# Column tiles for the second mixer's output products in a one-core encoder layer

## The reference, cut to what matters

```python
for direction, reverse in ((0, False), (1, True)):
    lam_bar = jnp.exp(lam * step)
    b_bar = ((lam_bar - 1.0) / lam)[..., None] * b_in
    bu = jnp.einsum('blgi,gpi->blgp', ugc, b_bar)
    _, states = lax.associative_scan(
        _diag_recurrence, (jnp.broadcast_to(lam_bar, bu.shape), bu), axis=1, reverse=reverse)
    y = y + jnp.real(jnp.einsum('blgp,gip->blgi', states, c_out))
y = jax.nn.gelu(y.reshape(bsz, seqlen, S5_WIDTH))
```

## Time and profile before

| what | value |
|---|---|
| median of 3 runs | 3546.41 us (3544.83 to 3548.12) |
| the profiled execution | 3543.74 us |
| its span, first to last instruction | 3542.0 us |
| PE busy over the span | 3101.9 us, 88% |
| the stage `s5_outputs`, PE's first to last product | about 1376.5 to 1551.1 us |

### The profile page before, as it was taken

One profiled execution on the slowest core, in us unless ns is written; L12 is line 12 of the kernel. 1 busy time (PEld: TensorE's weight loads), 2 busy tenths in 40 slices (PEclk: granted clock), 3 DMA queues, 4 the chain that ended last, 5 costly groups with the idle time before them and its releaser, 6 DMA issues. The chain is left out here.

```text
span 3542.0 us, 41193 instructions
## 1 busy us (share of the span) xinstructions
PE 3101.9 (88%) x13052; PEld 1420.7 (40%) x13052; DVE 1339.5 (38%) x2344; ACT 751.0 (21%) x1652; POOL 675.4 (19%) x699
## 2 busy tenths in 40 slices
PE   8999999968799743978999965999999999999990
PEld 3444444436566402544444423333333333333330
DVE  3134223447688787623333344111111111111116
ACT  1011111123489500111212210111111111111116
POOL 1000000003255202413222220111111111111113
PEclk9999999988899876999999977999999999999995
DMA  6111020145344421462232114434545446344237
GB/s 242 48 54 65 36 77 30 42 142 170 114 137 141 182 89 45 130 212 107 99 116 116 59 49 184 139 99 118 161 112 148 116 117 189 88 145 118 53 101 291
DMA packets 147269, 414.96 MB, mean 117 GB/s; under 512 B 14421, under 2 KB 58197, under 8 KB 138597
## 3 DMA queue, kind: packets, MB, share of 16 engines
q1 hardware_dynamic: 108888, 315.88, 25.3%
q0 software_dynamic: 17024, 58.73, 8.3%
q10 hardware_dynamic: 21266, 39.16, 3.0%
HBM read 889.26 MB, written 122.16 MB: 286 GB/s over the span
## 5 line engine op out<-in xcount | busy, mean ns | idle before, releaser
L2218 PE MATMUL bank<-wg,exp_ht 128*64 128x512 f32 x1792 | 408.0, 597 | 1.1 <-DVE exp_ht L2307 1.1
L2218 PE MATMUL bank<-wu,exp_ht 128*64 128x512 f32 x1792 | 406.2, 595 | 1.3 <-issue 1.3
L2238 PE MATMUL bank<-wd,exp_hid_t 128*64 128x512 f32 x1792 | 395.8, 594 | 0.8 <-issue 0.8
L1669 PE MATMUL bank<-mix_wo,mix_yt 128*128 128x512 f32 x768 | 347.1, 602 | 18.2 <-DMA mix_wr<-in_w_router 10.6
L2173 POOL DMA_INDIRECT v<-exp_out,exp_sink x112 | 158.4, 1414 | 1003.8 <-DVE exp_out L2326 734.2
L472 PE MATMUL bank<-w_in,pro_ht 128*128 128x512 f32 x768 | 337.4, 592 | 0.0
L472 PE MATMUL bank<-pro_ht,w_in 128*128 128x512 f32 x768 | 336.4, 593 | 0.9 <-ACT pro_ht L534 0.9
L2318 DVE SCALAR_TENSOR_TENSOR exp_scale<-exp_g,row_gate,exp_scale 128x1024 f32<-128x1024 f32 x56 | 71.9, 1284 | 488.4 <-ACT exp_scale L2281 488.4
L2238 PEld LDWEIGHTS bank<-wd,exp_hid_t 128*64 128x64 f32 x1792 | 129.6, 137 | 257.0 <-issue 257.0
L2218 PEld LDWEIGHTS bank<-wg,exp_ht 128*64 128x64 f32 x1792 | 124.4, 137 | 233.0 <-issue 226.4
L2218 PEld LDWEIGHTS bank<-wu,exp_ht 128*64 128x64 f32 x1792 | 124.0, 137 | 232.4 <-issue 225.8
(11 more groups left out here) (348 smaller groups left out, 3974.5 us busy)
## 6 DMA issues: line engine op xcount, KB each, us to landing
wg<-in_w_gate SPq DMA_DIRECT2D x112, 2048.0 KB
wu<-in_w_up SPq DMA_DIRECT2D x112, 2048.0 KB
wd<-in_w_down SPq DMA_DIRECT2D x112, 2048.0 KB
ada_wt<-in_w_ada SPq DMA_DIRECT2D x8, 2048.0 KB, 10.5
pro_xt<-in_x SPq DMA_DIRECT2D x6, 2048.0 KB, 9.8
mix_xt<-in_x SPq DMA_DIRECT2D x6, 2048.0 KB, 12.8
v<-mix_kept_v ACTq DMA_DIRECT2D x24, 512.0 KB, 2.6
h<-mix_h ACTq DMA_DIRECT2D x24, 512.0 KB, 3.5
```

The source lines that it names most:

```text
L1669: mul = pe.matmul(C.bank[2 + 2 * (a % 2) + q][:, :], yt[:, j, k, a * P:(a + 1) * P], wo[:, k, q * WIDE:(q + 1) * WIDE], start=k == 0, stop ...
L2218: mul = pe.matmul(bank[rows, :], ht[:, j, k, rows], of[:, s, k * DE:(k + 1) * DE], start=k == 0, stop=k == KT - 1)
L2238: mul = pe.matmul(bank[rows, :], hid_t[:, j, k, rows], wd[:, s, k * D + q * WIDE:k * D + (q + 1) * WIDE], start=k == 0, stop=k == KD - 1)
```

## The change

It moves outputs to other partitions of PSUM, and changes the order of some loops:

- `kernel_of`: direction 1 goes to partitions 32 to 47 instead of columns 256 to 511, so that the two directions lie in two column tiles of 32. The loops go over `r`, then `d`, then `g` (before: `d`, `r`, `g`).
- `kernel_lags` reads direction 1 from there.
- `output`, prompt: the outputs of both groups go to one bank, group 0 on partitions 0 to 63 and group 1 on partitions 64 to 127, two column tiles of 64. In L1445 the two groups then differ in rows and in columns of the array; in L1455 (all 128 rows) they differ in columns. L1455 goes over `k`, then `g` (before: `g`, then `k`), for the sample too.
- gelu reads the prompt's outputs from there.

```diff
+    COL = 32
+        def bank_rows(i, g, s):
+
+            return yb[i * 2][g * C_P:(g + 1) * C_P, TC:2 * TC] if s else yb[i * 2 + g][0:C_S, 0:TC]
...
-                        f, b = kernel_bank[g][0:CH5, 0:TC], kernel_bank[g][0:CH5, TC:2 * TC]
+                        f, b = (kernel_bank[g][d * COL:d * COL + CH5, 0:TC] for d in range(2))
...
-                        lag.done(dve.tensor_tensor(to[:, g, L0:L0 + CH5], kernel_bank[g][0:CH5, TC + L0:2 * TC], to[:, g, L0:L0 + CH5], ALU.add))
+                        lag.done(dve.tensor_tensor(to[:, g, L0:L0 + CH5], kernel_bank[g][COL:COL + CH5, L0:TC], to[:, g, L0:L0 + CH5], ALU.add))
...
-                    for d in range(2):
-                        for r in range(2):
+                    for r in range(2):
+                        for d in range(2):
                             for g in range(2):
-                                mul = pe.matmul(kernel_bank[g][0:CH5, d * TC:(d + 1) * TC], bs[half(g), j, r, d, :],
+                                mul = pe.matmul(kernel_bank[g][d * COL:d * COL + CH5, 0:TC], bs[half(g), j, r, d, :],
                                                 e[half(g), j, r, d, d * CH5:d * CH5 + TC], start=r == 0, stop=r == 1)
...
+                        to = [bank_rows(i, g, s) for g in range(2)]
                         for d in range(2):
                             for r in range(2):
                                 for g in range(2):
-                                    mul = pe.matmul(yb[i * 2 + g][0:n, s * TC:(s + 1) * TC], st[half(g), i, r, d, at:at + n],
+                                    mul = pe.matmul(to[g], st[half(g), i, r, d, at:at + n],
...
-                        for g in range(2):
-                            for k in range(HALF):
-                                mul = pe.matmul(yb[i * 2 + g][0:n, s * TC:(s + 1) * TC], ut[:, j, g, k, at:at + n], toe[:, j, g, k, :],
+                        for k in range(HALF):
+                            for g in range(2):
+                                mul = pe.matmul(to[g], ut[:, j, g, k, at:at + n], toe[:, j, g, k, :],
...
-                            act.activation(y[:, :, cols], yb[m % 2 * 2 + g][0:n, s * TC:(s + 1) * TC].rearrange("p (t i) -> p t i", t=T5),
+                            act.activation(y[:, :, cols], bank_rows(m % 2, g, s).rearrange("p (t i) -> p t i", t=T5),
```

## The result

The changed kernel took 3555.67 us in the median of 12 runs (3551.3 to 3558.78), against 3547.22 us for 12 runs of the kernel before (3543.3 to 3552.89). The ratio is 1.0022 with a 95% interval of 1.0014 to 1.0029: slower, by some 8 us. The forecast was no change, 3545 us, with a range of 3536 to 3556 us. The profiled executions are 3555.13 and 3543.74 us, 11.4 us apart. All of that lies in this stage, which took 186.0 us from PE's first product to its last instead of 174.4.

The account below looks back on a forecast made before the run. The prediction took the chain through DVE and the `toe` loads, not PE, as the bound: 5 us saved, about 4 us of clock losses, rounded to -1.5 from 3546.4, giving 3545 us, range 3536 to 3556.

Parts of the forecast that it names:

- the chain from T to the next A but one: DVE's `entering` and `kernel_lags`, store of `lags`, `toe` loads; with PE's A to T, 19.4 us per two turns.
- T: T(m): the moment the prompt's L1445 ends in turn m; DVE's `entering(m + 3)` starts there.
- A: A(m): the start of the sample's L1455 in turn m, which waits for the loads of `toe`.
- rival of one bank: Prompt's L1445: row halves can't write one bank together, 1.94 to 3.9 us; +13 us, 3559; chance 0.13 with slower reads.
- even waits: PE's waits for `toe` before A of even turns, where its saved time gathers: about 4.2 us each.
- The end of the stage: After T(13): last `kernel_lags` start moves up 1.85 us, last prompt L1455 saves 0.95.
- Half of the losses is the middle: -5 + 4 = -1 us: The sum: about 5 us earlier without clock losses, about 3 us later with all; rounded to -1.5 us.
- a loss was priced at 1.6 us from one row: Sample L1455 and prompt L1445 after a 3.97 us wait: 3.35 and 2.20 us against 1.97 and 1.94.
- slower reads: DVE's `kernel_lags` reading other partitions: up to 0.95 us per two-turn chain, some 6 to 8 us; chance 0.13 with one bank.
- T(0) was taken as fixed: End of turn 0's prompt L1445: it stays, as A(0) waited 3.97 us for its loads.
- nothing is lost behind 2.73 us: PE's groups after waits of 2.73 and 1.82 us were read as losing nothing to the lower clock.
- a sign that the prediction had named against itself: The forecast is wrong if the store at turn 8 costs A(9) much less than its earlier 5.64 us.

Follow-up runs that it names:

- the chain shortened: The full change with DVE doing `kernel_lags` before `entering` from turn 3 on, against the kernel before: 3534.42 us against 3546.64, ratio 0.9958.
- the prompt's outputs alone: Only the prompt's outputs in two column tiles of one bank, `kernel_of` and `kernel_lags` as before, against the kernel before: 3549.0 us against 3546.64, ratio 1.0005.
- the kernel before with lags first: The kernel before, without the change, with `kernel_lags` ahead of `entering` from turn 3 on, against the kernel before: 3542.29 us against 3547.16, ratio 0.9986.
- The filled wait: The full change plus eight unread products a turn before the wait for `toe`, against the kernel before: 3545.72 us against 3546.64, ratio 0.9998.
- the directions' half: Only the two directions' kernels in two column tiles, outputs as before, against the kernel before: 3554.35 us against 3546.64, ratio 1.0016.
- Shorter reads: Only the directions' kernels in column tiles, `kernel_lags` reading with one change of partition, against the kernel before: 3551.99 us against 3547.16, ratio 1.0015.
- half as much: The full change plus four unread products a turn before the wait for `toe`, against the kernel before: 3554.35 us against 3544.19, ratio 1.0023.

## Why the prediction was wrong

- *What bounds the stage* was right: the chain from T to the next A but one, not PE. Taking some 1.7 us a turn from PE didn't bring T(6) forward; with the chain shortened it did (50.1 us from T(0) to T(6), against 56.6 without the column tiles).
- *The parts.* Prompt L1455 was taken at 1.0 us and measured 1.08; L1431 at 0.95 to 1.0, measured 1.05. The prompt's L1445 was taken at 1.94, and it takes 1.94 or 1.95 in all turns without a wait. The rival of one bank fell: products that differ in rows and in columns overlap in one bank here as they did in two. For this form, then, the rule of the Trainium skill's page "TensorEngine Tiling (Array Packing)", section "Restrictions and Gotchas", by which that rival would have been the result, doesn't hold; row tiles that share their columns in one bank were not run.
- *Where the saved time goes* was right up to turn 7: even waits of about 4.2 us forecast, 4.40, 4.73 and 4.48 measured; 35 us of waiting forecast, 37.4 measured. The end of the stage, T(13) to the last product, came out as forecast too: 16.5 us instead of 19.0, 2.5 less (2.8 forecast).
- *The step that failed* is in the sum: "Half of the losses is the middle: -5 + 4 = -1 us". The losses of clock behind the waits were taken too small twice. First, not half of the waits but all seven of 3.28 us and more, from turn 2 on, were followed by slow products. Second, a loss was priced at 1.6 us from one row. In turns 2, 4 and 6 the two groups took 5.55, 6.71 and 5.59 us against 1.97 + 1.94 = 3.91: losses of 1.64, 2.80 and 1.68, together 6.1 us between T(0) and T(6). Even with all losses the sum only reached 3 us later, so a kernel slower by over 0.2% was forecast only from other causes, one bank or slower reads, with a chance of 0.13. One bank cost nothing, and the reads some 1 us of the 7.6. That 3555.67 lies just inside the range is luck.
- *DVE's reads* were taken at nothing, with a bound of 0.95 us in each chain of two turns. They cost 0.35: over three chains 1.05 us. With the 6.1 this is 7.2 of the 7.6 us by which T(0) to T(6) grew.
- *The stages of the loss.* By T, the profiled execution lost 2.6 us up to T(0), 7.6 to T(6), gained 0.5 to T(9), lost 4.4 to T(13), and gained 2.5 at the end: 11.6. T(0) was taken as fixed, and in these two executions it wasn't. The shorter `kernel_of(0)` and longer `kernel_lags(0)` made `kernel_of(1)` wait 4.77 us instead of 2.73, and the first output ran at the low clock (0.50). But how much of the 2.6 us the change makes isn't shown: the first sample L1445 group took 2.00 us in the profile of the kernel before and 2.88 to 3.57 us in the ten others, also in the two that have its `kernel_of`. In these three, `kernel_of(1)` waited the same 2.73 us, and took 1.90, 3.60 and 2.49 us:

```profile
1382.91 1.90 PE L1431 MATMUL bank<-out_e,out_bs 64*16 64x256 f32 x16 [2.73 <-DVE out_lags L1409]
...
1381.97 3.60 PE L1436 MATMUL bank<-out_e,out_bs 64*16 64x256 f32 x16 [2.73 <-DVE out_lags L1414]
...
1381.37 2.49 PE L1433 MATMUL bank<-out_e,out_bs 64*16 64x256 f32 x16 [2.73 <-DVE out_lags L1409]
```

These are the kernel before, the prompt's outputs alone, and the kernel before with lags first. So that nothing is lost behind 2.73 us, as the prediction read it from one row, held in one execution of three.
- *The store of outputs at turn 8* fell otherwise than forecast. A(9) waited 3.28 us instead of 5.64, a sign that the prediction had named against itself; but A(8) waited 6.51 us instead of 0.95. The store now starts 0.6 us behind the issue of turn 8's `toe` loads, and 8.6 us passed from that issue to A(8). Before, they were issued 3.4 us ahead of the store (1463.95 and 1467.35), and 6.9 us passed. From T(6) to T(9) this made no loss: 36.5 us instead of 37.0. The kernel before first, then SP's, ACT's and PE's rows of the changed one:

```profile
1470.81 1.97 PE L1455 MATMUL bank<-out_toe,out_ut 128*128 128x256 f32 x8 [0.95 <-DMA out_toe<-kernels]
...
1476.27 2.46 SPq L1348 DMA_DIRECT2D out_toe<-kernels  x4
...
1476.88 0.68 ACTq L1477 DMA_DIRECT2D yg<-out_ys  x1
...
1484.91 3.75 PE L1461 MATMUL bank<-out_toe,out_ut 128*128 128x256 f32 x8 [6.51 <-DMA out_toe<-kernels]
...
1497.74 2.67 PE L1461 MATMUL bank<-out_toe,out_ut 128*128 128x256 f32 x8 [3.28 <-DMA out_toe<-kernels]
```

- The filled wait settles the cause for the full change. Left open is whether and why the directions' half alone is slower than the prompt's half, 1.0016 against 1.0005: their intervals overlap. In the two profiles a part lies at the stage's end, where only the prompt's half saves: T(13) to the last product took 17.0 us with it, 18.6 with the directions' half and 19.0 before. Shorter reads showed no gain, and both halves have waits of 2 to 3 us, behind which products were slow or not.

## What to carry to other kernels

Before work is taken from an engine, ask on which side of the releasing point it lies. Work that runs after the point that starts the chain, beside the chain, isn't what bounds: taking it away shortens nothing, it only lengthens the wait at the chain's end. Here such a wait on TensorE wasn't free, since a wait of 3 us or more made the next products slow, and those lie in the chain; then saved work cost time, and useless work that filled the wait gave it back, while half as much did not. Shorten the chain first (here by an exchange of two calls on DVE, 5 us alone); the saving then counts (7 to 10 us more).

## What was not expected of the hardware

DVE and POOL slow each other here. In the kernel before, `entering` and POOL's copies of the states both start at T and run side by side: POOL's two 254-wide and 126-wide copies take 2.02 us, and L1389, which follows the L1388 of the earlier trace rows, takes 1.15 us. With `kernel_lags` first they run apart. POOL and DVE in order of time, in the kernel with lags first:

```profile
1415.12 0.97 POOL L1367 COPY out_st<-states 128x254 f32<-128x254 f32 x2 [6.43 <-PE bank L1453]
1416.03 0.96 POOL L1369 COPY out_st<-states 128x254 f32<-128x254 f32 x2
...
1419.97 0.71 DVE L1394 TENSOR_TENSOR out_t<-out_c,power_y 128x544 f32<-128x544 f32 x1
```

and in the kernel before:

```profile
1405.69 2.02 POOL L1362 COPY out_st<-states 128x254 f32<-128x254 f32 x2 [4.84 <-PE bank L1445]
1406.30 1.15 DVE L1389 TENSOR_TENSOR out_t<-out_c,power_y 128x544 f32<-128x544 f32 x1
```

The same copies take half, the same multiplication 0.71 us, and `entering` 4.25 us instead of 5.3. Not every instruction of DVE beside POOL is slower: L1388, which begins 0.03 us ahead of POOL's copies, takes 0.73 us, and 0.70 when alone. The Trainium skill's page "SBUF — State Buffer", section "Who interferes with whom", says that a DVE instruction with two SBUF inputs contends with a GpSimd instruction that reads SBUF; the rows of L1389 and of the copies agree.

A second finding is the price of reading PSUM from another first partition than the instruction before: about 0.1 us each, 0.43 instead of 0.33 us from one copy's start to the next. With four such changes, one and none the eight instructions of `kernel_lags` took 2.25, 2.02 and 1.90 us.
